# Ten projection chunks of the mixer in three fp32r passes, with the remainders made by GpSimd

## What is computed

```python
for l in range(DEPTH):
    proj = h @ w_in[l]
    rg_x, rg_gate, z, xbc, dt_raw, q, k, v = jnp.split(proj, SPLIT_POINTS, axis=-1)
    y_a = jax.nn.gelu(rg_gate) * rg_lru(causal_dwconv(rg_x, ...), ...)
    y_b = mamba2_group(z, xbc, dt_raw, ...)
    y_c = sliding_window_attention(q, k, v, attn_sinks[l])
    mix = jnp.concatenate([y_a, y_b, y_c], axis=-1) @ w_out[l]
    h = layer_norm(DN_ALPHA * h + mix, ln1_g[l], ln1_b[l])
    ffn = peer_ffn(h, peer_wq[l], peer_keys[l], peer_u[l], peer_v[l])
    h = layer_norm(DN_ALPHA * h + ffn, ln2_g[l], ln2_b[l])
```

## Time and profile before

| | before |
|---|---|
| median of 3 runs | 2832.52 us (2828.89 to 2837.93) |
| profiled execution | 2826.41 us |
| its span | 2824.8 us |
| mean granted TensorE clock | 0.988 of full speed |
| PE busy | 2719.9 us, 96% |
| DVE busy | 1852.2 us, 66% |
| ACT busy | 930.1 us, 33% |
| POOL busy | 339.0 us, 12% |

### The profile page before, as it was taken

One profiled execution on the slowest core, in us unless ns is written; L12 is line 12 of the kernel. 1 busy time (PEld: TensorE's weight loads), 2 busy tenths in 40 slices (PEclk: granted clock), 3 DMA queues, 4 the chain that ended last, 5 costly groups with the idle time before them and its releaser, 6 DMA issues.

```text
span 2824.8 us, 46538 instructions
## 1 busy us (share of the span) xinstructions
PE 2719.9 (96%) x17136; PEld 2481.0 (88%) x17136; DVE 1852.2 (66%) x4104; ACT 930.1 (33%) x1983; POOL 339.0 (12%) x409
## 2 busy tenths in 40 slices
PE   8999999999998999998999999999999989999998
PEld 5888888778888888998899999977889989999998
DVE  6888888656665786779944445448857996444553
ACT  4222223334674565412611110036742153111001
POOL 0000000000000000003911112100000175111120
PEclk9999999999999999999999999999999999999999
DMA  7233333223323234377579999932345955999994
GB/s 307 102 120 129 118 117 127 73 89 110 120 75 105 105 120 149 132 272 306 185 302 369 368 386 419 353 134 105 120 149 182 372 192 214 373 372 368 395 415 167
DMA packets 86337, 608.88 MB, mean 216 GB/s; under 512 B 9584, under 2 KB 9968, under 8 KB 13744
## 3 DMA queue, kind: packets, MB, share of 16 engines
q1 hardware_dynamic: 60480, 420.23, 40.0%
q0 software_dynamic: 25712, 186.79, 16.8%
HBM read 605.93 MB, written 1.05 MB: 215 GB/s over the span
## 4 chain that ended last, share of the span: by engine, by line
PE 79%; DVE 12%; DMA 3%; issue 3%; DVEq 2%; ACT 2%; ACTq 0%; POOL 0%; POOLq 0%
PE bank L2527 19%; PE bank L495 10%; PE bank L497 10%; PE bank L496 10%; PE bank L2519 9%; PE bank L2468 4%; PE bank L1681 2%; PE bank L2504 2%; DMA arena<-in_experts,arena 2%; PE bank L2491 2%; DVE res L2576 2%; DVE arena L2571 1%; DVE arena L2830 1%; PE bank L998 1%; PE bank L987 1%
## 5 line engine op out<-in xcount | busy, mean ns | idle before, releaser
L2527 PE MATMUL bank<-arena,wring 128*128 128x176 f32 x4096 | 633.1, 314 | 6.3 <-DVE arena L2854 3.0
L2527 PEld LDWEIGHTS bank<-arena,wring 128*128 128x128 f32 x4096 | 616.7, 190 | 11.5 <-issue 4.8
L479 DVE TENSOR_TENSOR peer_r<-wring,peer_r 128x512 fp32r<-128x512 f32 x440 | 296.4, 698 | 214.7 <-ACT peer_r L474 211.7
L495 PE MATMUL bank<-h_r,peer_r 128*128 128x512 f32 (+1 forms) x1088 | 396.8, 365 | 4.4 <-DVE h_r L509 3.4
L497 PE MATMUL bank<-h_r,peer_r 128*128 128x512 f32 (+1 forms) x1088 | 384.2, 353 | 0.0
L2584 POOL DMA_INDIRECT arena<-in_experts,arena x160 | 170.9, 1068 | 1762.6 <-DVE arena L2802 1002.8
L474 ACT ACTIVATE peer_r<-wring 128x512 fp32r<-128x512 f32 x440 | 266.7, 628 | 232.1 <-PE bank L497 227.5
L496 PE MATMUL bank<-h_r,peer_r 128*128 128x512 f32 (+1 forms) x960 | 333.6, 348 | 0.0
L2571 DVE SCALAR_TENSOR_TENSOR arena<-arena,res 128x1024 f32<-128x1024 f32 x128 | 156.8, 1225 | 229.3 <-DMA arena<-in_experts,arena 228.0
L2468 PE MATMUL bank<-res,wring 128*128 128x176 f32 x1920 | 288.1, 313 | 4.0 <-ACT arena L2626 4.0
L2468 PEld LDWEIGHTS bank<-res,wring 128*128 128x128 f32 x1920 | 286.6, 190 | 5.4 <-issue 4.8
(11 more groups left out here) (424 smaller groups left out, 4064.2 us busy)
## 6 DMA issues: line engine op xcount, KB each, us to landing
wring<-in_w_peer SPq DMA_DIRECT2D x256, 1024.0 KB, 7.5
wring<-in_w_proj SPq DMA_DIRECT2D x34, 1024.0 KB, 4.8
wring<-in_w_hy SPq DMA_DIRECT2D x32, 1024.0 KB, 5.1
arena<-in_w_ada POOLq DMA_DIRECT2D x16, 1024.0 KB, 5.1
wring<-in_w_out SPq DMA_DIRECT2D x16, 1024.0 KB, 4.8
wring<-in_w_ada SPq DMA_DIRECT2D x8, 1024.0 KB, 10.1
wring<-in_w_hyout SPq DMA_DIRECT2D x8, 1024.0 KB, 4.8
wring<-in_w_q SPq DMA_DIRECT2D x8, 1024.0 KB, 4.8
```

Source lines behind the costliest of these rows:

```text
L479: v.tensor_tensor(SPLIT[:, buf, 1, :], raw_quarter(name, i, j, q), SPLIT[:, buf, 0, :].bitcast(F32), ALU.subtract).then_inc(split_lo, 1)
L495: pe.matmul(out_ap, w_hi, x_hi, start=start, stop=False, **kw)
L2527: mm = pe.matmul(expert_sum(k), w[:, k * P:(k + 1) * P], GP[:, par, :], start=False, stop=True, skip_group_check=True)
```

## The change

The chunks 5 to 9 are multiplied by `proj_split` too. ScalarE makes their high parts: three quarters of the next chunk ahead of the copy of the present one, the fourth behind it. Their remainders are made by GpSimd, in a new function that runs ahead of `peer_pool` in each layer; it marks the chunk done for the ring, and counts in a semaphore of its own. `lo_of` takes these quarters out of the count that DVE's remainders keep. For chunk 10 the high parts of the first three quarters stand where all four stood, and the fourth behind the copy of chunk 9.

```diff
-SPLIT_CHUNKS = (3, 4, *range(10, 17))
+SPLIT_CHUNKS = range(3, 17)
+POOL_CHUNKS = range(5, 10)
...
+        def lo_of(name, i, q):
+
+            layers = {"out0": 1, "wq0": 1, "proj1": 1, "out1": 2, "wq1": 2}.get(name, 0)
+            within = name[:4] == "proj" and q >= UNITS * SPLIT_CHUNKS.index(POOL_CHUNKS[-1] + 1)
+            return unit_of(name, i, q) - UNITS * len(POOL_CHUNKS) * (layers + within)
...
             for q in range(UNITS):
-                pe.wait_ge(split_lo, proj_unit(l, j, q) + 1)
+                if j in POOL_CHUNKS:
+                    pe.wait_ge(pool_lo, UNITS * (len(POOL_CHUNKS) * l + POOL_CHUNKS.index(j)) + q + 1)
+                else:
+                    pe.wait_ge(split_lo, lo_of(f"proj{l}", 0, UNITS * SPLIT_CHUNKS.index(j) + q) + 1)
...
+        def proj_pool(pool, l):
+            for j in POOL_CHUNKS:
+                for q in range(UNITS):
+                    pool.wait_ge(split_hi, proj_unit(l, j, q) + 1)
+                    pool.tensor_tensor(SPLIT[:, q, 1, :], raw_quarter(f"proj{l}", 0, j, q),
+                                       SPLIT[:, q, 0, :].bitcast(F32), ALU.subtract).then_inc(pool_lo, 1)
+                pool.drain().then_inc(chunk_done[slot_of(f"proj{l}", 0, j)[0]], 1)
...
-            proj_chunk(pe, l, 5)
+            proj_split(pe, l, 5)
...
-                proj_chunk(pe, l, 6 + m0)
+                proj_split(pe, l, 6 + m0)
...
-            proj_chunk(pe, l, 8)
+            proj_split(pe, l, 8)
...
-            proj_chunk(pe, l, 9)
+            proj_split(pe, l, 9)
...
             root_scalar(act, l)
+            proj_hi(act, l, 5, range(3))
             proj_out(act, l, 4)
+            proj_hi(act, l, 5, (3,))
             exps_scalar(act, l, 0)
             for m0 in range(3):
+                proj_hi(act, l, 6 + m0, range(3))
                 proj_out(act, l, 5 + m0)
+                proj_hi(act, l, 6 + m0, (3,))
                 turned_scalar(act, l, m0)
                 silu_scalar(act, l, m0)
                 exps_scalar(act, l, m0 + 1)
+            proj_hi(act, l, 9, range(3))
             proj_out(act, l, 8)
+            proj_hi(act, l, 9, (3,))
             turned_scalar(act, l, 3)
-            proj_hi(act, l, 10, range(4))
+            proj_hi(act, l, 10, range(3))
             silu_scalar(act, l, 3)
             proj_out(act, l, 9)
+            proj_hi(act, l, 10, (3,))
             segment_scalar(act, l, 0)
...
             for l in range(DEPTH):
+                proj_pool(pool, l)
                 peer_pool(pool, l)
```

More of the change, by code:

```diff
@@ L515, in chunk3 @@
             for q in quarters:
-                c = unit_of(name, i, UNITS * j + q)
-                pe.wait_ge(split_lo, c + 1)
+                pe.wait_ge(split_lo, lo_of(name, i, UNITS * j + q) + 1)
                 if parts is not None and kt == 16:
@@ L1637, in program @@
         prj_all = sem("prj_all")
+        pool_lo = sem("pool_lo")
         dt_mm = sem("dt_mm")
@@ L1924, in out_tensor @@
                 k, half = OUT_K[2 * j + q // 2], q % 2
-                pe.wait_ge(split_lo, unit_of(name, 0, UNITS * j + q) + 1)
+                pe.wait_ge(split_lo, lo_of(name, 0, UNITS * j + q) + 1)
                 for tt in range(2):
```

## The result

The changed kernel takes 2861.97 us (median of 6 runs, 2856.51 to 2866.51) against 2830.87 of the kernel before (6 runs, 2828.82 to 2837.93) on the same chip: ratio 1.011, 95% interval 1.0095 to 1.0125. That is 31 us slower, where 5.3 were forecast, and outside the range. The profiled execution took 2860.73, its span 2859.1 against 2824.8.

A forecast was written before the change was run, and what follows sets the result against it. PE bounds the kernel behind 1017 us; before that the mixer's chain runs largely over DVE and ScalarE. 2 x 1.8 for the copies' chain plus 1.7 for PE's clock gave 2832.5 + 5.3 = 2837.8 us, 8-in-10 range 2825 to 2852.

The forecast's parts named there:

- So GpSimd gives way and DVE loses 0.01 us: Where GpSimd's remainders run beside DVE's two-input operations: GpSimd's are stretched, DVE loses only 0.01 us.
- DVE blocked: Rival, steps 6 to 9: remainders hold the port, DVE's two-SBUF-input operations wait; 10 to 21 us per layer; chance 0.17.
- ScalarE's order: Attention loop: three copies between exponentials and eviction delay conv(1) and conv(2) by 0.97 us each; step 11.4 us.
- conv(0): First convolution of the attention loop: DVE starts at 972.4 instead of 972.84, 0.4 us gained.
- second sums: Broadcast sums behind chunk 9: PE's operand comes at 1018.4 instead of 1016.59, +1.8 us per layer.
- PE's wait ahead of them: PE idle after chunk 9, before the broadcast sums: 2.8 us instead of 1.2.
- The scans: DVE's scans ahead of conv(0): the prediction counted no cost for their meeting GpSimd's remainders.
- PE's clock: Behind the wait ahead of the broadcast sums: lower clock loses 1.7 us, taken for one layer of two; bounds 0 and 3.4.
- the copies' chain: From ScalarE's copies through convolutions and chunk 9 to the broadcast sums: +1.8 us per layer.
- A second place: Lower PE clock inside the attention loop, where PE idles more but has slack: no cost counted.
- Remainders: GpSimd's 20 subtractions per layer: 1.29 to 2.9 us each, 9.8 us per chunk taken, in time for the eviction.
- PE's saving counts: Rival: each of the ten three-pass chunks brings 1.3 us, 13 in all, giving 2819.5 us; chance 0.08.

The follow-up runs named there:

- experiments 4 to 9: Kernel before with unneeded GpSimd subtractions (4), only ScalarE's copies (5), or other GpSimd forms (6 to 9): 2865.34, 2843.7, 2844.94, 2835.77, 2845.15, 2850.68 us.
- experiment 1: The changed kernel without GpSimd's 40 subtractions, with passes, copies and order kept: 2841.24 us, ratio 1.0036.
- Experiment 6: The kernel before with unneeded GpSimd tensor_scalar operations of 128x512, one SBUF input each: 2844.94 us, ratio 1.0051.
- experiment 7: The kernel before with unneeded GpSimd memsets of 128x512, which read nothing: 2835.77 us, ratio 1.0019.
- experiment 2: The changed kernel with GpSimd's subtractions held back, chunk 5's until the first scores, chunk 6+m's until convolution m is done: 2868.0 us.
- experiments 8 and 10: 8: the kernel before with unneeded GpSimd subtractions cut into 128x128, 2845.15 us; 10: the changed kernel with its own subtractions cut likewise, 2844.08 us.
- experiment 4: The kernel before with 20 unneeded GpSimd subtractions of 128x512 per layer, at about the change's moments: 2865.34 us, ratio 1.0131.
- experiment 5: The kernel before with only ScalarE's added copies, 16 per layer, results unused: 2843.7 us, ratio 1.0052.

## Why the prediction was wrong

- **The step that failed** is "So GpSimd gives way and DVE loses 0.01 us", and with it the chance of 0.17 for the rival "DVE blocked". It rested on the earlier trace rows, a GpSimd tensor_scalar of 128x128, carried over to a tensor_tensor of 128x512. By experiments 4 to 9 both halves of that step matter: twice the inputs (0.81 against 1.34 us at the same size) and four times the length (0.52 against 1.34). In the changed kernel DVE loses 0.87 us per meeting, and without the subtractions the kernel is about 20 us faster (experiment 1). The earlier trace rows were read rightly, and showed a form for which the cost is near nothing. The rival had the mechanism and, in its lower half (2858 to 2868), the size; its own words, that it decides as soon as a meeting costs over 0.1 us, were met nearly nine times over (1.35 - 0.48 = 0.87).
- The rule that spoke against the change, in the Trainium skill ("SBUF — State Buffer", Who interferes with whom), was the better guide. It says that the one that comes second blocks for the whole of the other's instruction. The trace of after agrees: 1.35 us beside GpSimd operations of 1.36, while the product that started at 973.00, 0.09 us ahead of GpSimd's group, took 0.69 as alone. Experiment 6 does not agree: beside a GpSimd tensor_scalar of 1.48 us DVE's operation was through in 0.81, and the measurement decides. The same section says that a GpSimd instruction which only writes does not collide with a DVE instruction that has two SBUF inputs; experiment 7 agrees, 1.23 us across three memsets. It names tensor_scalar among the operations that can take the shared pair by a mode of their own: the two of 1.17 us in experiment 2 and the one of 1.00 us in experiment 7 agree. Since the wait is for one instruction, the short pieces of experiments 8 and 10 follow from the rule as well; the prediction did not draw that from it.
- **ScalarE's order**: right. Step 11.4 forecast, 11.34 without the subtractions and with the copies alone; conv(0) -0.42 against -0.40; second sums +1.8 against +1.91; PE's wait ahead of them 2.8 against 2.8. In the changed kernel these are buried: the copies move the step from 13.7 (experiment 4, layer 0) to 13.96 only.
- **The scans** were missing in the list of what meets GpSimd. They lose 4.06 us, of which 2.2 reach conv(0) (+1.77 instead of -0.42).
- **PE's clock**: behind the wait ahead of the second sums the place was right and the size was off by a factor of two: 1.5 us in both layers, 3.0, where one in two, 1.7, was taken. With the copies' chain (2 x 1.9) that is 6.8; experiment 1 measured 11 with an interval of 6 to 14. The rest is inside the interval. A second place was put at nothing, because PE "has the slack to be slower" in the loop: in the changed kernel the slow stretch of the loop reached into chunk 9, which has no slack, another 1.6 us per layer. In experiment 1 chunk 9 has full clock in both layers, so this part went with the subtractions here; but it is slow in one layer of experiment 5 too, so it is not theirs alone.
- **Remainders**: 1.55 us each, inside the bounds of 1.29 and 2.9, and in time. My picture was inverted: I let GpSimd wait for DVE, 9.8 us per chunk. It took 5.9, and DVE waited.
- **"PE's saving counts"** fell: experiments 1 and 5 differ by less than their intervals.

The account of the 31 us, about: 20 for the subtractions, with what they cost in clock (experiment 1), 11 for the copies' place and the clock behind it. The mixers of the profiled executions would give 27 and 7; the difference lies in stretches outside them and stays open.

## What to carry to other kernels

Work given to an idle engine is free only if it shares nothing with the engine that sets the pace; before GpSimd is given fp32 work beside DVE operations with two SBUF inputs, look for a row of that very form and length side by side, and if there is none, let the rule that speaks against it have the larger chance. If it must be done there, cut it short: four pieces took 42% more GpSimd time per chunk here and gave back some 17 of 31 us. And an engine's saved work counts only on the chain, and there TensorE's lower clock can take it back in the next stage.

## What was not expected of the hardware

- The price of a meeting follows the length and the inputs of the GpSimd operation, not the bytes moved: 1.34, 0.80 and 0.52 us for subtractions of 128x512, 128x256 and 128x128 (0.48 alone), and 0.81 beside a tensor_scalar of 128x512 that lasts longer than the subtraction.
- A GpSimd memset left operations with two SBUF inputs alone and held up a DVE tensor_scalar: 1.00 us instead of 0.41.
- A tensor_scalar of two columns took 1.17 us instead of 0.23, so of what was measured here the smallest DVE operation lost most by share.
- TENSOR_TENSOR_SCAN meets it as well, 0.66 to 1.70 us; a reduction and operations with an input in PSUM did not.
- TensorE kept full clock behind a wait of 1.19 us in one kernel and fell to half behind the same wait in another, and even the two layers of one execution differed. What tells them apart stays open.
